# The first layer's input projection: straight products with quarter-wise loops, or Strassen products with the heads unrolled

## What is computed

```python
proj = x @ w_in                     # (1024, 1024) @ (1024, 3 * 2048 + 16)
xm, z, o_pre = proj[..., :E_A], proj[..., E_A:2 * E_A], proj[..., 2 * E_A:3 * E_A]
xc = silu(causal_dwconv(xm, conv_w, conv_b))        # 4 taps over the tokens
q, k, v = per head: xch @ w_q, xch @ w_k, xmh @ w_v
h = mlstm_chunkwise(q, k, v, log_i, log_f)          # 8 chunks of 128 tokens
hb = sigmoid(o_pre) * layer_norm(h) * norm_g + skip * xc
x = layer_norm(alpha * x + (hb * silu(z)) @ w_out)
```

## Time and profile before

| what | us |
|---|---|
| median of 3 runs (lowest to highest) | 1562.37 (1562.05 to 1564.95) |
| time of the profiled execution | 1562.89 |
| its span, first to last instruction | 1561.1 |
| PE busy in it | 1511.4 (97%) |
| DVE, ACT, POOL busy | 1017.9, 570.3, 194.6 |
| mean granted TensorE clock | 0.993 of full |
| one head of the loop (heads 1 to 6) | 91.2 |

### The profile page before, as it was taken

The page is one execution under the profiler, slowest core; times in us unless marked ns, Lnnn a source line. Parts: engine busy times, 40 slices in busy tenths (PEclk is TensorE's granted clock), DMA queues, the critical chain, the costliest instruction groups (busy, mean ns, idle before and its releaser), DMA issues.

```text
span 1561.1 us, 20244 instructions
## 1 busy us (share of the span) xinstructions
PE 1511.4 (97%) x6994; PEld 1253.6 (80%) x6994; DVE 1017.9 (65%) x1557; ACT 570.3 (37%) x878; POOL 194.6 (12%) x161
## 2 busy tenths in 40 slices
PE   7999999999999999999999999979999999889998
PEld 6888888888888888888888888758887777678886
DVE  4867677776767767677744214486777778788424
ACT  5632424233242423325434224464333333343200
POOL 3213122120312212031200000000000000000001
PEclk9999999999999999999999999999999999999999
DMA  5113112021311202131463333331222222263121
GB/s 179 51 33 96 41 48 75 26 84 37 94 40 47 74 27 83 38 94 47 174 207 116 97 100 95 118 102 66 83 81 78 72 81 81 80 271 113 41 90 54
DMA packets 113965, 133.14 MB, mean 85 GB/s; under 512 B 7128, under 2 KB 89192, under 8 KB 113392
## 3 DMA queue, kind: packets, MB, share of 16 engines
q1 hardware_dynamic: 112832, 132.28, 26.1%
q10 hardware_dynamic: 1072, 0.07, 0.0%
HBM read 102.93 MB, written 29.39 MB: 85 GB/s over the span
## 4 chain that ended last, share of the span: by engine, by line
PE 87%; DVE 9%; ACT 2%; issue 2%; DMA 1%; DVEq 0%; POOL 0%; SPq 0%; ACTq 0%; POOLq 0%
PE wide L1853 22%; PE wide L1855 22%; PE wide L1854 22%; PE ps_intra L1976 2%; PE ps_inter L1979 2%; PE ps_state L1981 2%; DVE blk L1617 1%; PE ps_inter L1853 1%; PE ps_state L1853 1%; PE ps_inter L1854 1%; PE ps_inter L1855 1%; PE ps_s L1853 1%; PE ps_state L1854 1%; PE ps_state L1855 1%; PE ps_intra L1853 1%
## 5 line engine op out<-in xcount | busy, mean ns | idle before, releaser
L1853 PE MATMUL wide<-x_hi,w_hi 128*128 128x512 f32 x768 | 307.1, 400 | 0.0
L1855 PE MATMUL wide<-x_hi,w_lo 128*128 128x512 f32 x768 | 299.7, 390 | 0.0
L1854 PE MATMUL wide<-x_lo,w_hi 128*128 128x512 f32 x768 | 298.7, 389 | 0.0
L1855 PEld LDWEIGHTS wide<-x_hi,w_lo 128*128 128x128 f32 x768 | 144.1, 188 | 31.2
L1854 PEld LDWEIGHTS wide<-x_lo,w_hi 128*128 128x128 f32 x768 | 144.5, 188 | 28.0
L1853 PEld LDWEIGHTS wide<-x_hi,w_hi 128*128 128x128 f32 x768 | 144.4, 188 | 27.1
L855 POOL TENSOR_TENSOR w_lo<-w_raw,w_hi 128x1024 fp32r<-128x1024 f32 x48 | 118.6, 2470 | 305.9 <-ACT w_hi L932 304.8
L1854 PE MATMUL wide<-xa,blk 128*128 128x512 f32 x384 | 149.4, 389 | 0.0
L1853 PE MATMUL wide<-xb,blk 128*128 128x512 f32 x320 | 126.2, 394 | 16.6 <-DVE zz L1688 14.6
L1855 PE MATMUL wide<-xb,blk 128*128 128x512 f32 x320 | 125.0, 391 | 0.0
L893 POOL TENSOR_SCALAR small<-small 128x1 f32<-128x1 f32 x15 | 4.1, 273 | 728.5 <-ACT gate_b L1103 478.6
(11 more groups left out here) (320 smaller groups left out, 3383.0 us busy)
## 6 DMA issues: line engine op xcount, KB each, us to landing
w_raw<-in_mlstm_w_in SPq DMA_DIRECT2D x48, 512.0 KB, 3.7
y_heads<-f_buf SPq DMA_DIRECT2D x32, 256.0 KB, 2.0
wu_raw<-in_pool_w_u SPq DMA_DIRECT2D x32, 256.0 KB, 2.7
wm_raw<-in_mlstm_w_out SPq DMA_DIRECT2D x16, 512.0 KB, 5.1
folded<-stage SPq DMA_DIRECT2D x32, 256.0 KB, 2.8
a_raw<-in_pool_w_z SPq DMA_DIRECT2D x16, 512.0 KB, 3.3
a_raw<-folded SPq DMA_DIRECT2D x16, 512.0 KB, 3.5
y_rows<-zz SPq DMA_DIRECT2D x16, 512.0 KB, 2.7
```

The source lines that it names most:

```text
L1853: pe.matmul(dst, a[0], b[0], start=first, stop=False, skip_group_check=more)
L1854: pe.matmul(dst, a[0], b[1], start=False, stop=False, skip_group_check=more)
L1855: return pe.matmul(dst, a[1], b[0], start=False, stop=last, skip_group_check=more)
```

## The change

The projection of the first layer is done as 24 pairs of Strassen products: pair p is head p // 3 and kind p % 3 (x, z or o), 256 columns of the weights by 1024 tokens, and has seven products (numbers 1 to 7) of four tiles of the depth in place of eight, 12 passes each. The host lays out x transposed in four quarters (`x_t`) and the weights by head (`by_head`); the transpositions of x on TensorE are gone, and so is the head loop on all engines. The quarters of x are summed and split once at the start (8 sums, 14 splits, each of 128x1024). For each pair VectorE makes four sums of weight quarters (`in_sum`), seven lower parts (`in_low`) and three joins (`in_join`); ACT makes seven upper parts (`in_high`), three snapshots (`in_snapshot`) and one copy (`in_upper_right`). GpSimd no longer subtracts lower parts; it masks the decay row once per head (one `affine_select` of 1024 columns), sets ones and takes the two powers.

A "tick" is what ACT and VectorE do after one product. Four blocks (`RING_A`) are in flight: in the tick of product t they prepare the block of product t + 4, after the tick's own snapshot, join, sums and chunk, and before its extras. The gates are 60 passes, issued after product (1, 1). Chunks 1 and 3 of a head's core follow the last two products of its o pair, chunks 0, 2, 4, 5, 6 and 7 products of the next head's x and z pairs.

Moved from VectorE to ACT: the first tap, the skip term, the decay (with the mask folded in), k's weighting and the normalisation (`norm_head`, four instructions of 128x256 for each half). On VectorE the gated output has three instructions for each quarter in place of two (`y_part`), and the z gate is written into `z_buf`, which is the previous head's until `y_part` has read it: the snapshots of z wait for `y_sum`. The lower part of the q, k and v weights moves from GpSimd to VectorE (`low_qkv`), and one product of 128x1024 for the decayed q (`weighted_q`) takes the place of eight scaled sums. SyncE's queue has the same weight loads in larger pieces, one more row per head (`wi_rows`, 512 KB broadcast), and loads x again for the residual during the output projection. In the last head chunks 2 to 7 lie between the first folds, of which six come ahead of the output projection in place of three. `Y_RING` is 4 in place of 6.

The core of the diff (the remainder renames, moves buffers, or writes out what is told above):

```diff
+PAIRS_A = 3 * HEADS
+RING_A = 4
+PRODUCTS_A = [(0, 1), (0, 2), (0, 6), (0, 7), (0, 5),
+              *((p - back, q) for p in range(1, PAIRS_A)
+                for back, q in ((0, 1), (1, 4), (0, 2), (1, 3), (0, 6), (0, 7), (0, 5))),
+              (PAIRS_A - 1, 4), (PAIRS_A - 1, 3)]
+AT_A = {pq: i for i, pq in enumerate(PRODUCTS_A)}
+TICKS_A = len(PRODUCTS_A)
...
+CHUNK_AFTER = {(X_OF, 1): 0, (X_OF, 2): 2, (X_OF, 6): 4, (X_OF, 7): 5, (X_OF, 5): 6, (Z_OF, 1): 7}
+def chunk_after(p, q):
+    h, kind = p // 3, p % 3
+    if kind == O_OF and q in (4, 3):
+        return h, {4: 1, 3: 3}[q] if h < HEADS - 1 else {4: 0, 3: 1}[q]
+    if h and (kind, q) in CHUNK_AFTER:
+        return h - 1, CHUNK_AFTER[kind, q]
+    return None
...
+            def in_snapshot(t):
+                p, q = PRODUCTS_A[t]
+                h, kind = p // 3, p % 3
+                at, (j, n) = {1: (1, (0, 0)), 6: (2, (1, 0)), 5: (3, (1, 1))}[q]
+                act.wait_ge(in_prod, t + 1)
+                if (p, q) == (1, 1):
+                    act.wait_ge(gw_lo, 2)
+                if h and kind == Z_OF:
+                    act.wait_ge(y_sum, 4 * h - 4 + {1: 1, 6: 2, 5: 4}[q])
+                link(act, act.activation(in_target(p, j, n), wide[:, p % 2, :], ACT.Copy), in_snap, 3 * p + at)
...
+                if c + 1 < NC - 1:
+                    weighted_k(h, c + 1)
+                take_num(h, c)
+                if c + 2 < NC:
+                    decay(h, c + 2)
+                if c == 5:
+                    norm_head(h, 0)
...
+                if kind == X_OF:
+                    if q == 1 and h:
+                        tanh_o(h - 1, 1)
+                    elif q == 2 and h:
+                        tanh_o(h - 1, 2)
+                    elif q == 3:
+                        first_tap(h, 0)
+                elif kind == Z_OF:
+                    if q == 2:
+                        if h:
+                            norm_head(h - 1, 1)
+                        first_tap(h, 1)
+                    elif q == 6:
+                        tanh_conv(h, 1)
+                    elif q == 5:
+                        high_xc(h, 1)
+                    elif q == 4:
+                        tanh_conv(h, 0)
+                        tanh_z(h, 0)
+                        skip_term(h, 1)
+                    elif q == 3:
+                        high_xc(h, 0)
+                        skip_term(h, 0)
+                        high_xm(h, 0)
+                        tanh_z(h, 1)
+                elif q in (4, 3):
+                    if h == HEADS - 1:
+                        tanh_o(h, {4: 1, 3: 2}[q])
+                elif q == 6:
+                    high_xm(h, 1)
+                    tanh_o(h, 0)
+                    tanh_z(h, 2)
+                elif q == 7:
+                    high_qkv(h)
...
+                elif q == 5:
+                    decay(h, 0)
+                    for i in range(4):
+                        take_v(h, i)
+                    for i in range(2):
+                        take_q(h, i)
+                    for i in range(2):
+                        take_k(h, i)
+                    weighted_k(h, 0)
+                    decay(h, 1)
...
+            def tick_a(t):
+                p, q = PRODUCTS_A[t]
+                if q in (1, 6, 5):
+                    in_snapshot(t)
+                elif q == 3:
+                    in_upper_right(t)
+                in_high(t + RING_A)
+                if chunk_after(p, q):
+                    chunk(*chunk_after(p, q))
+                extras(p, q)
+                gate_steps(p, q)
...
+            def in_join(p, q):
+                at, (j, n), op, s, done = {2: (2, (0, 0), ALU.add, 1, in_c11), 4: (3, (1, 0), ALU.subtract, 2, in_c21),
+                                           5: (3, (1, 1), ALU.subtract, 3, in_c22)}[q]
+                dve.wait_ge(in_prod, AT_A[p, q] + 1)
+                dve.wait_ge(in_snap, 3 * p + s)
+                dst = in_target(p, j, n)
+                dve.tensor_tensor(dst, wide[:, at, :], dst, op).then_inc(done, 1)
...
+            def extras(p, q):
+                h, kind = p // 3, p % 3
+                if kind == X_OF:
+                    if q == 5 and h:
+                        y_of(h - 1, 0)
+                    elif q == 4 and h:
+                        norm_scale(h - 1, 1)
+                        y_of(h - 1, 1)
+                    elif q == 3:
+                        for i in range(1, CONV):
+                            tap(h, 1, i)
+                elif kind == Z_OF:
+                    if q == 6:
+                        if h:
+                            y_of(h - 1, 2)
+                        tap(h, 0, 1)
+                    elif q == 7:
+                        gate_conv(h, 1)
+                        if h:
+                            y_of(h - 1, 3)
+                    elif q == 5:
+                        tap(h, 0, 2)
+                    elif q == 3:
+                        gate_out_z(h, 0)
+                        low_xc(h, 1)
+                elif q == 1:
+                    tap(h, 0, 3)
+                elif q == 2:
+                    gate_conv(h, 0)
+                elif q == 6:
+                    low_xm(h, 0)
+                    low_xc(h, 0)
+                elif q == 7:
+                    low_xm(h, 1)
+                    gate_out_z(h, 1)
+                    low_qkv(h)
+                elif q == 5:
+                    gate_out_z(h, 2)
+                    gate_out_z(h, 3)
...
+                    weighted_q(h)
+                    weighted_s(h, 0)
...
+            def tick_a(t):
+                p, q = PRODUCTS_A[t]
+                if q in (2, 4, 5):
+                    in_join(p, q)
+                if q == 5 and p + 1 < PAIRS_A:
+                    in_sum(p + 1, 0)
+                elif q == 1 and p:
+                    in_sum(p, 1)
+                    in_sum(p, 2)
+                elif q == 4 and p + 1 < PAIRS_A:
+                    in_sum(p + 1, 3)
+                if chunk_after(p, q):
+                    chunk(*chunk_after(p, q))
+                in_low(t + RING_A)
+                extras(p, q)
+                gate_steps(p, q)
...
+            def in_bank_free(p, q):
+                h, kind = p // 3, p % 3
+                if q == 1:
+                    if p >= 2:
+                        pe.wait_ge(in_c12, p - 1)
+                    if kind == X_OF and h:
+                        pe.wait_ge(q_taken, 2 * h - 1)
+                elif q in (6, 5, 3):
+                    pe.wait_ge(in_snap, 3 * p + {6: 1, 5: 2, 3: 3}[q])
+                elif q == 2:
+                    if p:
+                        pe.wait_ge(in_c11, p)
+                    if kind == X_OF and h:
+                        pe.wait_ge(q_taken, 2 * h)
+                elif q == 7 and p:
+                    pe.wait_ge(in_c21, p)
+                elif q == 4:
+                    pe.wait_ge(in_c22, p + 1)
+            def in_product(i):
+                p, q = PRODUCTS_A[i]
+                pe.wait_ge(in_lo, i + 1)
+                if p == 0:
+                    pe.wait_ge(ax_lo, operand_ready[q])
+                in_bank_free(p, q)
+                dst = wide[:, {2: 2, 7: 3, 4: 3}.get(q, p % 2), :]
+                for t in range(4):
+                    mm = split(dst, [inb[:, i % RING_A, part, tile(t)] for part in range(2)],
+                               [v[:, t, :] for v in operands[q]], t == 0 and q in (1, 2, 7), t == 3, q not in (1, 2, 7))
+                mm.then_inc(in_prod, 1)
...
+            for t, (p, q) in enumerate(PRODUCTS_A):
+                h, kind = p // 3, p % 3
+                in_product(t)
+                if chunk_after(p, q):
+                    chunk(*chunk_after(p, q))
+                if (p, q) == (1, 1):
+                    for n in (10, 14):
+                        pe.wait_ge(ax_lo, n)
+                    pe.wait_ge(gw_lo, 2)
+                    gates()
+                elif (p, q) == (2, 2):
+                    gate_columns()
+                if h:
+                    if (kind, q) == (X_OF, 5):
+                        turn_head(h - 1, 0)
+                    elif (kind, q) == (Z_OF, 1):
+                        turn_head(h - 1, 1)
+                    elif (kind, q) == (X_OF, 3):
+                        for m in (2, 3):
+                            turn_head(h - 1, m)
...
-            head(0, FIRST, True)
-            with pe.Fori(1, HEADS) as h:
-                head(h, LATER, False)
```

More of the change, by code:

```diff
@@ L313, in build @@
             stage = sM("stage", [P, STAGES, HALF])
+            places = [*range(0, 32, 8), *range(40, 136, 8)]
+            wm_raw, wm = ([v[places.index(kb)] for kb in WM_KB] for v in (wm_raw, wm))
         with ExitStack() as own:
@@ new lines, in in_upper_right @@
+            def in_upper_right(t):
+                p, q = PRODUCTS_A[t]
+                h, kind = p // 3, p % 3
+                act.wait_ge(in_prod, t + 1)
+                if h and kind == Z_OF:
```

(35 more changed lines are left out.)

1726 lines of the change are left out of this document (879 added, 847 removed).

## The result

| what | before | after | forecast |
|---|---|---|---|
| median, us | 1562.2 | 1689.1 | 1644 (1568 to 1668) |
| ratio, 95% interval | | 1.081 (1.079 to 1.083) | 1.05 |
| one head of 1 to 6 | 91.2 | 102.4 | 98.3 |
| TensorE, VectorE, ACT busy in it | 91.2, 64.6, 31.4 | 88.4, 67.4, 54.9 | 83, 71, 52 |
| first product, gates' end, heads' end | | 11.7, 62.4, 863.0 | 10, 60, 840 |

The change makes the kernel 8% slower. The direction was forecast; the time lies 21 us beyond the upper end of the range, and 45 beyond the forecast. (The sum of the forecast puts the heads' end at 834; the 840 in its last part forgot that six chunks, 9.3 us, now stand behind the heads.)

A forecast was written before the change was run, and what follows sets the result against it. TensorE bounds the kernel before; afterwards it waits for VectorE's and ACT's bunched queues. Terms: -65.4 + 10.8 + 25.3 + 107 + 4 = +81.7 on 1562.4, giving 1644 us, 8-in-10 range 1568 to 1668.

The forecast's parts named there:

- what TensorE does: In each head, 252 passes in place of 288: 65.4 us less over 8 heads, a head of 83.0 without waits.
- the three places: Stretches of a steady head where TensorE waits for the in-order VectorE and ACT queues: 15.3 us a head, 107 for seven.
- the third: At q, k and v: TensorE has only O5 (2.9) while ACT and VectorE finish the split weights: 4.7 us of waits.
- the second: From Z4 to O5: TensorE has 13.6 us of work, VectorE and ACT together 18.0: 4.4 us of waits.
- the first place: From the end of X5 to Z4: VectorE's queue takes 32.7 us against TensorE's 26.0: 6.7 us of waits.
- 29.6 of one queue: VectorE's listed work from X5's tick to the join of Z5, before 1.5 of lateness and 1.6 of waits for ACT.
- The likeliest case: Whole kernel slower by 60 to 95 us, around 1644, own range 1620 to 1665; chance 0.60.
- The rival that had one: Waits also cost clock: v and q run slowly, 1.5 us a head and some at the start, 1658; chance 0.13.
- the 4 that I had added for the last head: In the last head, the fold's first weights are prepared ahead of q's product on VectorE: 4 us more.
- The start and the first head: Start 10.8 us later, gates' end 60.7; first head 25.3 us of waits, mostly behind the gates' chain.
- what I cost at nothing: Reordered folds and chunks, output projection's loads, SyncE's added traffic and written-out heads: no cost, at most blocks late once.
- the landings: Output projection's blocks loaded four ahead: three blocks of 4.1 us against landings of 2 to 5, costed at nothing.

The follow-up runs named there:

- e11: e3 and e6 with gated output, taps, normalisation and (from head 1) skip term cut to one column each, results wrong: 1547.4 us, ratio 0.989 to the kernel before.
- e3: Changed kernel with the split of the q, k and v weights moved in heads 1 to 7 from O7's tick to X2's and X6's: 1640.6 us, ratio 1.048.
- e4: Changed kernel with the twelve VectorE instructions of a head's gated output cut to one column each: 1650.9 us, ratio 1.053.
- e9: Changed kernel with o and z gates multiplied together early, leaving two VectorE instructions per quarter after the turns: 1661.3 us, ratio 1.060.
- e10: e3, e6, e7 and e9 together, plus two ACT instructions (x's first-half rounding, a z tanh) moved behind O6's snapshot: 1618.6 us, ratio 1.035.
- e6: Changed kernel with GpSimd's masking of the decay row held back until product O6 of the same head has ended: 1681.4 us, ratio 1.076.
- e7: Changed kernel with X5's join placed after the sum, chunk and lower part in VectorE's queue, heads 1 to 7: 1687.4 us, ratio 1.079.
- e1: Changed kernel with idle TensorE time filled by unread matmuls ahead of the turns, Z4, O5 and v: 1671.8 us, ratio 1.067.
- e5: e3 with unread filler matmuls in TensorE's remaining waits, ahead of the turns, Z4 and O5: 1641.1 us, ratio 1.049.
- e12: Changed kernel with unread filler matmuls ahead of three second-layer products that wait for VectorE's join: 1680.4 us, ratio 1.073.
- e8: Changed kernel with the first head's gates' chain cut to one column per instruction, all instructions and waits in place: 1677.8 us, ratio 1.073.

## Why the prediction was right or wrong, point by point

**Right: what TensorE does.** 83.0 a head without waits; e11 shows 83.1.

**Right: the three places.** From the end of X5 to Z4 34.5 us (forecast 32.7), from Z4 to O5 18.2 (18.0), from O5 to v 7.4 (7.6), each ended by the instruction that was named. e3 removes the third, e4 and e9 shorten the first, e10 among other things the second (16.5), and in e11 only 0.4 before O5 is left. No run takes the second by itself.

**Mis-sized: the first place, by 1.8.** 0.7 is the masking on GpSimd beside the taps, which I had priced at 1.3 each; e6 shows it. The trace of the kernel before could have told me: 46 of its 48 taps take 1.28 or 1.29 us, and two take 3.3, beside subtractions on GpSimd.

```profile
58.98 3.30 DVE L1363 SCALAR_TENSOR_TENSOR tmp_a<-xm,cols,tmp_a 128x1024 f32<-128x1024 f32 x1
```

```profile
58.63 2.57 POOL L855 TENSOR_TENSOR w_lo<-w_raw,w_hi 128x1024 fp32r<-128x1024 f32 x1 [9.29 <-ACT w_hi L932]
```

These two raise the mean of the row to 1.37, and not waits for a register of the loop, as I had read it.

The rest isn't separated by a run. It shows as longer pieces of the ACT and GpSimd chain: the power 1.45 where the kernel before has 1.01, the first tap 1.24 where I had 1.06, the join's wait 2.2 where I had 1.5. And "29.6 of one queue" was not the whole cause: e4 and e7 show a second chain of nearly the same length.

**The step that failed: the waits were priced as if TensorE lost nothing but the wait.** The likeliest case had no clock in it. The rival that had one priced it at 1.5 for each head, and gave it 0.13. It was true, and cost 2.0 in each head (e1), though 5.4 us of half clock can be seen there. Its argument that the rest is swallowed by the next wait was right (e1, e5), but the chance that I gave it was too small. With the 1.8 of the first place and some small gaps, a head comes to 102.4 in place of 98.3: 29 us for seven heads, less the 4 that I had added for the last head and that didn't come, so 25. In all, the clock is some 28 of the 45 us: 14 in seven heads, up to 7.7 in the first and 6.4 in the second layer, both told below. Without them the time would be about 1661 (an estimate from these numbers), inside the range.

**The start and the first head: 5 us too short.** Gates' end 62.4 (forecast 60.7), end of head 0's k 138.2 (133.2). The first head's waits are 5.1 + 8.8 + 0.9 + 1.7 + 4.4 = 20.9, in place of 25.3; in their stead came 7.7 of half clock behind (1, 5), (1, 4) and v (the 3 us behind (1, 4) have a granted clock of 0.50), and of small gaps. The 7.7 are what the difference leaves; no run fills these waits.

**Failed: "what I cost at nothing".** From the heads' end on the kernel takes 824.1 us. Before it took 800.0, and 9.3 of chunks were moved there; 14.8 are new. The second layer is 6.4 of them, by clock alone: nearly the same waits are followed by half clock once before the change and three times after it, and e12 takes all of it away. The six folds, six chunks and two turns ahead of the output projection take 30.4, of which 26 are work: waits of 1.3 and 2.4 for lower parts, where 0.7 was before. The output projection takes 4.9 more than the same work did before, 4.2 of them in four waits for the y blocks of the last pass. The first of the four: the block has landed, but ACT rounds it only behind the copy of a fold, for which it waits itself.

```profile
1084.88 0.60 ACT L1276 ACTIVATE stage<-ps_state 128x512 f32<-128x512 f32 x1 [2.27 <-PE ps_state L2076]
1085.51 0.42 ACT L1286 ACTIVATE ym<-ym_raw 128x256 fp32r<-128x256 f32 x1
```

```profile
1086.51 0.50 PE L2074 MATMUL wide<-wm,ym 128*128 128x512 f32 x1 [0.84 <-DVE ym L1807]
```

I had looked for trouble in the landings. That four blocks in flight in place of six are the reason is likely, not shown. These two are read from the trace, and weren't tried.

In sum 5 + 25 + 15 = 45, which is the miss.

**The range.** Its upper end, 1668, stood on waits without a price for the clock behind them. The case in which all the waits are followed by half clock wherever TensorE leads, in the heads, the start and the second layer, is the one that came.

## What to carry to other kernels

- Where an engine gets less to do and another one more, add up the other's queue between two fixed events of the first, place by place, and don't stop at the first chain that is too long: the next one decides what a cure is worth (e7: 2.2 us of idle time filled, 0.2 gained in a head).
- Price TensorE's waits (2.5 to 4.4 us here) with what comes behind them: some 2 us lost to half clock where TensorE leads next, nothing where it will wait again. Expect that stages that weren't touched move by it.
- A step whose inputs have long been there (the split of the q, k and v weights) should stand where its engine has slack. Two instructions moved gave 49 us, of which 42 can be read in the heads; no operation was saved.

## What was unexpected on the hardware

- The same wait of 2.94 us, before and behind the same instructions, is followed by a first matmul of 0.47 us in one program and of 0.77 in another; one of 4.20 was followed by 0.47 in four of the programs above (e3, e5, e6, e8), by 0.62 to 0.77 in the others that have it. A wait of 2.54 in the heads was followed by half clock (0.55 over 3 us).
- A single GpSimd instruction slows VectorE's beside it (0.69 to 1.65 us), and the masking of 1.5 us alone made the way from the turns to Z4 0.7 longer (17.6 against 16.9).
